# Fifty-eight FFN tiles whose weight distance, weight interleave and column order differ from tile to tile

## What is computed

```python
h = rmsnorm(x, norm_ffn_pre[l])
up = causal_dwconv(h @ w_up[l].astype(dt), ffn_conv_w[l])      # w_up: 1024 x 5632
gate, val = jnp.split(up, 2, axis=-1)
f = (jax.nn.silu(gate) * val) @ w_down[l].astype(dt)
x = x + rmsnorm(f, norm_ffn_post[l])
```

## Time and profile before

| | |
|---|---|
| median of 3 runs | 3190.34 us (3190.27 to 3190.47) |
| profiled execution | 3190.44 us |
| its span in the trace | 3189.1 us |
| TensorE (PE) busy in the span | 3169.5 us (99%), 14964 matmuls |
| granted TensorE clock | full (2.4 GHz) in all slices |

### The profile page before, as it was taken

How to read it: one execution, slowest core, us unless ns; L and a number is a source line. 1 busy time by engine, 2 the same in 40 slices (tenths; PEclk the granted TensorE clock), 3 DMA queues, 4 the chain that set the end, 5 groups by cost and what they waited for, 6 DMA issues and landing times.

```text
span 3189.1 us, 37007 instructions
## 1 busy us (share of the span) xinstructions
PE 3169.5 (99%) x14964; PEld 2654.6 (83%) x14964; DVE 1835.7 (58%) x2469; ACT 1243.9 (39%) x1866; POOL 396.0 (12%) x293
## 2 busy tenths in 40 slices
PE   8999999999999999999999999999999999999999
PEld 7888888888888888888888888888888888888887
DVE  6875456665687545656557543447545754345744
ACT  3332334344333233434445422236534442224642
POOL 0201212210020121211011000110012000011001
PEclk9999999999999999999999999999999999999999
DMA  4322223235442222323532222222232132222222
GB/s 167 116 99 93 99 93 112 94 132 188 139 125 93 99 93 100 106 97 119 194 125 78 97 99 87 97 86 98 97 122 87 67 104 94 86 99 95 92 94 101
DMA packets 100232, 339.71 MB, mean 107 GB/s; under 512 B 12288, under 2 KB 12544, under 8 KB 99296
## 3 DMA queue, kind: packets, MB, share of 16 engines
q1 hardware_dynamic: 96736, 322.76, 29.8%
q0 software_dynamic: 3184, 14.06, 1.3%
q10 hardware_dynamic: 144, 0.52, 0.1%
HBM read 326.29 MB, written 2.10 MB: 103 GB/s over the span
## 4 chain that ended last, share of the span: by engine, by line
PE 97%; DVE 1%; issue 1%; ACT 0%; DMA 0%; POOL 0%; POOLq 0%
PE ps L500 96%; PE ps L605 1%; PE ps L844 0%; DVE r L1427 0%; DVE wl L1417 0%; DMA X<-x_in 0%; POOL sm L2020 0%; ACT f L1265 0%; DVE h L1560 0%; DVE sm L1853 0%; PE ps L555 0%; DVE f L1553 0%; DVE f L1803 0%; DVE f L1863 0%; DVE r L1835 0%
## 5 line engine op out<-in xcount | busy, mean ns | idle before, releaser
L500 PE MATMUL ps<-h,wh 128*128 128x512 f32 (+1 forms) x5824 | 1702.5, 376 | 2.2 <-DVE h L1560 1.8
L500 PEld LDWEIGHTS ps<-h,wh 128*128 128x128 f32 x5824 | 1066.8, 189 | 199.3 <-issue 4.6
L500 PE MATMUL ps<-h,wl 128*128 128x512 f32 (+1 forms) x2912 | 1093.2, 375 | 0.0
L1417 DVE TENSOR_TENSOR wl<-raw,wh 128x1024 fp32r<-128x1024 f32 (+3 forms) x596 | 751.8, 1272 | 319.6 <-ACT wh L957 318.7
L957 ACT CAST wh<-raw 128x1024 fp32r<-128x1024 f32 (+3 forms) x596 | 595.9, 1008 | 720.1 <-PE ps L500 718.3
L500 PEld LDWEIGHTS ps<-h,wl 128*128 128x128 f32 x2912 | 548.7, 188 | 98.8
L500 PE MATMUL ps<-r,wh 128*128 128x512 f32 x1632 | 503.8, 390 | 0.0
L500 PEld LDWEIGHTS ps<-r,wh 128*128 128x128 f32 x1632 | 305.2, 188 | 62.7
L500 PE MATMUL ps<-r,wl 128*128 128x512 f32 x816 | 317.5, 389 | 0.0
L1032 ACT CAST r<-f 128x512 fp32r<-128x512 f32 x186 | 114.6, 620 | 511.9 <-DVE f L1756 148.5
L500 PE MATMUL ps<-wh,r 128*128 128x512 f32 x960 | 302.6, 390 | 0.3
(11 more groups left out here) (152 smaller groups left out, 2085.9 us busy)
## 6 DMA issues: line engine op xcount, KB each, us to landing
raw<-wst SPq DMA_DIRECT2D x544, 512.0 KB, 3.3
raw<-wst SPq DMA_DIRECT2D x48, 320.0 KB, 2.8
f<-gains POOLq DMA_DIRECT2D x6, 1024.0 KB, 5.2
raw<-wst SPq DMA_DIRECT2D x16, 384.0 KB, 3.0
f<-f SPq DMA_DIRECT2D x72, 64.0 KB, 2.0
f<-tab POOLq DMA_DIRECT2D x16, 256.0 KB, 5.0
r<-r SPq DMA_DIRECT2D x32, 128.0 KB, 2.3
X<-x_in SPq DMA_DIRECT2D x4, 512.0 KB, 8.4
```

The lines of the kernel that those rows point to most:

```text
L500: return e.matmul(o, a, b, start=start, stop=stop, skip_group_check=True)
L1417: e.tensor_tensor(l[:, 0:WIDTH[c]], raw[:, c % NRAW, 0:WIDTH[c]], h[:, 0:WIDTH[c]].bitcast(F32), ALU.subtract).then_inc(*lo_cut.up(("lo", c)))
```

## The change

High and low weights now lie in one tensor `ws` with four slots of 2 x 1024 + 64 numbers. By default the high part is at the start of a slot and the low part right behind it. 2112 is a multiple of 64, so the distance stays 0 for every tile that is not in the table `READ`.

`READ` gives 58 of the 80 tiles three things: `turns`, `past` and an order. They are all 40 tiles of block 0 (j = 2 to 21) and the first 18 of block 1 (j = 2 to 10).

- `past` moves the parts by 0 to 56 numbers: the distance.
- `turns` interleaves the two parts: the high ones on even places and the low ones on odd places, so a weight load, the cast and the subtraction each take every second number.
- the order (e, u) cuts the 512 positions into u strips and streams e numbers of each strip in turn (`paced`). The moving operand and the PSUM output are both addressed in that way, so each result lands where it did.

| tiles | turns | distances | order |
|---|---|---|---|
| 6 | no | 4, 8, 12, 24, 40, 56 | plain |
| 10 | yes | 0, 4, 8, 12, 16, 24, 32, 40, 48, 56 | plain |
| 28 | no | 0, 16, 32, 48 for each of six orders; 0, 8, 16, 48 for (16, 2) | (32,2) (64,2) (128,2) (16,4) (32,4) (8,2) (16,2) |
| 14 | yes | 0, 32 for each order | the same seven |

So 24 tiles are turned, 42 have an order of their own, and 7 keep distance 0 without turns. The number and sequence of instructions and their waits are unchanged on every engine; operand shapes and addresses differ.

```diff
-WAY = 48
+WAY, SLOT = 48, 2 * CH + 64
+ORDERS = [(32, 2), (64, 2), (128, 2), (16, 4), (32, 4), (8, 2), (16, 2)]
+WAYS = [(False, d, None) for d in (4, 8, 12, 24, 40, 56)] + [(True, d, None) for d in (0, 4, 8, 12, 16, 24, 32, 40, 48, 56)]
+WAYS += [(False, d, o) for o in ORDERS[:-1] for d in (0, 16, 32, 48)] + [(False, d, (16, 2)) for d in (0, 8, 16, 48)]
+WAYS += [(True, d, o) for o in ORDERS for d in (0, 32)]
+READ = dict(zip((NAME[f"{_l}/{_n}{_j}"] for _l in (0, 1) for _j in range(2, NF) for _n in ("upg", "upv")), WAYS))
...
+def paced(a, order):
+
+    return a if order is None else a.rearrange("p (u c e) -> p c u e", u=order[1], e=order[0])
...
-        wh = sb("wh", [P, WAY + NSP * CH], F32R)
-        wl = sb("wl", [P, NSP * CH], F32R)
+        ws = sb("ws", [P, WAY + NSP * SLOT], F32R)
...
-            n = RING[c] % NSP * CH
-            return wh[:, WAY + n:WAY + n + CH], wl[:, n:n + CH]
+            turns, past, _ = READ.get(c, (False, 0, None))
+            n = WAY + RING[c] % NSP * SLOT + past
+            if turns:
+                both = ws[:, n:n + 2 * CH].rearrange("p (n two) -> p n two", two=2)
+                return both[:, :, 0], both[:, :, 1]
+            return ws[:, n:n + CH], ws[:, n + CH:n + 2 * CH]
...
-            def three(o, ah, al, bh, bl, start, stop):
+            def three(o, ah, al, bh, bl, start, stop, order=None):
+                o, bh, bl = (paced(a, order) for a in (o, bh, bl))
                 mm(o, ah, bh, start, False)
                 mm(o, ah, bl, False, False)
                 return mm(o, al, bh, False, stop)
...
-                group(o, h, l, [k * P for k in range(len(xs))], xs).then_inc(
+                group(o, h, l, [k * P for k in range(len(xs))], xs, order=READ.get(NAME[name], (0, 0, None))[2]).then_inc(
```

More of the change, by code:

```diff
@@ L511, in weights, with group @@
                 return split_at(c)
-            def group(o, h, l, cols, xs, start=True, stop=True):
+            def group(o, h, l, cols, xs, start=True, stop=True, order=None):
                 for i, (c, (xh, xl)) in enumerate(zip(cols, xs)):
-                    last = three(o, h[:, c:c + P], l[:, c:c + P], xh, xl, start and i == 0, stop and i == len(cols) - 1)
+                    last = three(o, h[:, c:c + P], l[:, c:c + P], xh, xl, start and i == 0, stop and i == len(cols) - 1,
+                                 order)
                 return last
```

## The result

The changed kernel takes 3203.18 us (five runs, 3201.46 to 3203.21) against 3190.27 us for the kernel before in the same comparison. The ratio is 1.0039, with a 95% interval of 1.0024 to 1.0054. It is slower, by 12.9 us; I had forecast 7.1. The median lies inside the range of 3183 to 3215, and 0.2 us above the forecast case's own range of 3193 to 3203. The profiled execution took 3201.46 us, 11.0 us over that of before.

A forecast was written before the change was run, and what follows sets the result against it. TensorE was taken as the bound, by its matmuls' start-to-start distance. To the profiled 3190.44 us came +7.0 for disturbed placing and 0 for turned loads, seams and cast: 3197.4 us, range 3183 to 3215.

The forecast's parts named there:

- forecast case: A lost rhythm in the matmuls of the 58 tiles: 3197.4 us, own range 3193 to 3203; chance 0.42.
- The bound: TensorE, never idle in the 58 tiles' stretches: time is number of matmuls times start-to-start distance, plus some 1%.
- Term 1: Distance, turns and order disturb the settled placing of 1392 matmuls, 5.0 ns each: +7.0 us (-16.3 to +9.3).
- Term 3: Seams between runs in the streams of 42 ordered tiles: 0 taken, +9.9 us at one column's time each.
- Term 2: Turned weight loads in 24 tiles, 576 loads: 0 taken as likeliest, upper bound +7.7 us.
- Term 4: Cast and subtraction into every second place stay off the path: 0 us; +29 us over 24 tiles without cover.
- The two readings of the 13.3 ns: Each matmul's excess over its columns: fixed for changing weights, or from stream and next weight load meeting in SBUF.
- A: Rival: nothing in SBUF placing matters; 3190.4 us, +-1; chance 0.22.
- B: Rival: distance 0 is not cheap, other distances or slower orders hide the load; 3174 or 3182 us; chance 0.12.
- port rule: Two independent SBUF read ports on TensorE: loading next weights takes no bandwidth from the running matmul, so no distance matters.
- C: Rival: seams in ordered streams and turned weight loads cost; 3206 to 3215 us; chance 0.19.
- D: Rival: interrupted PSUM writes halve the rate in 42 ordered tiles; +215 us, 3405; chance 0.05 together with cast on path.

The follow-up runs named there:

- e2: Changed kernel with the 58 tiles' distances alone, nothing turned and all streams in plain order: 3196.32 against 3190.72 us, 1.0018.
- e9: The changed kernel once more, unaltered, for a second profile: 3202.99 against 3191.05 us, 1.0036.
- e6: Changed kernel with the orders of 42 tiles alone, all at distance 0, none turned: 3197.90 against 3190.60 us, 1.0023.
- e3: First survey, other table: 65 FFN tiles, one pattern each (distances, load and stream steps; b: activations shifted alone or with weights), other tiles plain: 3207.92 us.
- e5: Second survey, tile by tile: 32, 64 or 96 weight columns loaded, streams back to front, shifted or standing activations, other orders: 3201.39 us.
- e7: Third survey, tile by tile: only operand or only output permuted, standing or shifted activations, or fewer columns streamed: 3151.83 us.
- e4: Kernel before with WAY = 0 in place of 48, all ring weights at distance 16: 3259.55 against 3190.72 us, 1.0218.
- e8: Changed kernel's layout, all full tiles plain at distance 0, only the 24 early 256-column tiles at distance 16: 3186.61 against 3190.51 us, 0.9988.

## Why the prediction was right, and where it was not

**The bound** was read rightly. No wait came, PE stayed at 100% in both stretches, and the result is 1392 matmuls times a longer start-to-start time. That unlisted tiles would stay at 5.44 us held, from the second tile behind the change on; the first takes 5.46.

**Term 1**, 5.0 ns for a tile that has lost its rhythm, was right in that another place changes the rhythm. The plain tiles took 6.6 ns more, and e2 gives 5.7 on the mean over its distances. For the distances alone my estimate would have been 43 x 24 x 5.0 = 5.2 us, and e2 shows 5.9. But its size was taken from six matmuls that had not settled yet, and that is not what happens: the tiles do settle, each pattern in a rhythm of its own, from 226.7 to 243.6 ns, which e9 repeats. That 5.0 lies near the mean of the distances is luck. It was wrong to put the tiles with an order under the same 5.0 ns: in the changed kernel runs of 64 and 128 cost what their distance costs, and runs of 8 cost 16.6 ns.

**Term 3 was mis-sized**: I took seams as free beyond term 1. Orders alone cost 7.4 us for 42 tiles (e6), 7.4 ns per matmul. Nor is the unit that I used for the upper bound, one column's time per seam, what happens. Runs of 128 and 64 cost 0, of 32 cost 10.0, of 16 13.3, of 8 16.7 ns per matmul, while the seams go 3, 7, 15, 31, 63. With the same 31 seams, (16,4) takes 231.1 at distance 0 and (16,2) 240.0. Of the 4.5 us between my 7.0 and the 11.5 of the tiles, 4.2 are in the 42 tiles with an order (9.2 us, where I had 5.0), and 0.3 in the 16 others (2.3 for 1.9).

**Term 2**, turned weights at no price of their own, held on the mean: the ten turned plain tiles cost 1.33 us, and 1.15 at the same distances without turns (e2). A turned tile and a plain one of the same distance differ by +6.5 ns at 0, +4.0 at 48, -2.8 at 16, -3.9 at 24. **Term 4** held: the cast of turned tiles is 7% longer and the subtraction not at all, both hidden. After, then before, in the stretch of the ten turned plain tiles (minimum, median and maximum ns):

```profile
L975 ACT CAST ws<-raw x10: 1037/1107/1121, 514.7 to 565.1; 128x1024 fp32r<-128x1024 f32 x10
```

```profile
L957 ACT CAST wh<-raw x11: 1034/1039/1042, 514.4 to 568.8; 128x1024 fp32r<-128x1024 f32 x11
```

**The two readings of the 13.3 ns.** I wrote that the stream and the load meet. Half of it stands: the cost depends on where the load lies to the stream (e3, b), and it vanishes when the stream stands still (e3, e5, e7). The other half, that the time is paid for what the load reads, fell with the single-number load and the 32-column load, which at distance 0 cost more than a full one. What the runs show is that reading a moving float32r stream of 512 columns costs some 11 ns or more beyond a standing one, and that the place of the weights shifts this, at distance 0 to the best value seen. They don't show why, and no run streams without a weight load beside each matmul, so whether a stream alone would pay the 11 ns is not known. That the 13.3 ns was one amount per matmul, as I read rows 5, is wrong too: e7 has 16.6 to 20.0 at 448 to 496 columns. Tiles settle into repeating patterns whose means are often whole steps of 3.3 ns apart (226.7, 230.0, 233.3, 236.7, 240.0), which I can't explain. That stays open.

**Rivals.** A fell (e2). B fell for 512 columns: none of the plain and turned distances tried at the full stream is under 226.7. It holds for 256 columns, where distance 16 gives 113.3 or 117.8 for 120.0, and for 448; I had not looked there. The port rule of the Trainium skill ("TensorE: Matmul & The Clock Gate", Part 2) needs a limit: by where the weights lie, a matmul takes up to 8.3 ns longer here (235.0 at distance 7, e5). The outcome lies between the forecast case and C: the median is 5.8 us above my 3197.4 and 2.8 us under the lower end of C, 3206. C's sign, 5.8 us or more, stands in the six tiles with runs of 8 (5.84) and in one turned tile with runs of 16 (5.81). Its half about seams was right, but not with a price per seam; its half about turned loads was not. D fell with the result and in e7.

## What to carry to other kernels

When TensorE is busy all the time, read the start-to-start time of its matmuls and not their durations, and compare it with columns over clock: the rest can depend on the address of the weights relative to the activations. Here 48 numbers of padding are worth 69 us of 3190 (e4). Settle the distance for each stream length apart, since 512 columns want 0 and 256 want 16, and begin the stream at a multiple of 8 numbers. Permuting the output of a matmul cost nothing here in runs of 2 or more, but stream the operand in runs of 64 numbers or more; and let one kernel try many patterns, one per tile, which gave some 60 readings for the price of one run.

## What was not expected of the hardware

- A float32r stream of every second number takes 451 ns for 512 columns, twice the columns' time (e3). The Trainium skill ("SBUF — State Buffer", Specifications) has two accesses per 16-byte line as enough for full bandwidth, and every second float32 number is two per line. For this stream they are not enough; loads of every second number did keep pace, at 231.5 to 233.3 ns in e3.
- At distance 0 a weight load of 32 columns makes the matmuls slower than one of 128: 231.5 against 226.7 (e5).
- With weights and activations shifted alike by one number, a matmul takes 237.7 ns, 11 more than with neither or with both shifted by 8 (e5).
- An output in runs of 2 numbers costs nothing (e7).
- The time of a tile can depend on the tile before it: distance 4 settled at 233.3 or at 226.7 (e2), and 256 columns at distance 16 at 113.3 or 117.8 (e8).
